# Sample attention of a hybrid decoder: key transposes placed between low passes, ten blocks loaded early, and three orders rewritten

## The reference

```python
s = jnp.einsum('bqhd,bkhd->bhqk', qi, k, preferred_element_type=jnp.float32) * scale
s = s + fi.transpose(0, 2, 1)[..., :, None] - fk_t[..., None, :]
mask = k_pos[None, :] <= pi[:, None]
s = jnp.where(mask, s, -jnp.inf)
p = jax.nn.softmax(s, axis=-1)
return jnp.einsum('bhqk,bkhd->bqhd', p.astype(v.dtype), v)
```

## Time and profile before

| | |
|---|---|
| median of 3 runs | 3514.9 us (3512.66 to 3516.16) |
| the profiled execution's own time | 3511.37 us |
| its span, first to last instruction | 3509.6 us |
| mean granted TensorE clock | 0.984 |
| `third_pass` of the first and the last chunk | start 2182.0 and 2962.4 us |
| busy share of the span | PE 96%, DVE 63%, ACT 51%, POOL 47% |

### The profile page before, as it was taken

The page is one execution under the profiler, slowest core; times in us unless marked ns, Lnnn a source line. Parts: engine busy times, 40 slices in busy tenths (PEclk is TensorE's granted clock), DMA queues, the critical chain, the costliest instruction groups (busy, mean ns, idle before and its releaser), DMA issues. The chain is left out here.

```text
span 3509.6 us, 54504 instructions
## 1 busy us (share of the span) xinstructions
PE 3369.2 (96%) x17111; PEld 2664.7 (76%) x17111; DVE 2194.4 (63%) x3610; ACT 1782.2 (51%) x3705; POOL 1663.9 (47%) x1239
## 2 busy tenths in 40 slices
PE   7899999999999999998999998999999998899999
PEld 6678887788787878886677676777777776778787
DVE  3425566777555556554777773888888887544432
ACT  4411222554423474645677776777777775311222
POOL 2411314153455354210688876777777777222100
PEclk9999999999999999998999999999999999999999
DMA  7878787888888887888011115999999996544422
GB/s 263 314 223 280 227 262 250 275 309 282 268 272 267 280 279 255 250 243 229 13 29 45 43 37 179 345 345 345 347 346 344 347 352 238 207 162 165 145 87 84
DMA packets 426005, 810.17 MB, mean 231 GB/s; under 512 B 97741, under 2 KB 119157, under 8 KB 425738
## 3 DMA queue, kind: packets, MB, share of 16 engines
q1 hardware_dynamic: 413650, 799.67, 68.3%
q10 hardware_dynamic: 11520, 5.12, 0.5%
q0 software_dynamic: 576, 2.10, 0.2%
HBM read 674.11 MB, written 132.67 MB: 230 GB/s over the span
## 5 line engine op out<-in xcount | busy, mean ns | idle before, releaser
L1495 PE MATMUL prj_z_ps<-prj_w_hi,prj_h_ring 128*128 128x512 f32 x1792 | 724.2, 404 | 11.1 <-DMA prj_h_ring<-hops_scratch 6.6
L1497 PE MATMUL prj_z_ps<-prj_w_hi,prj_h_ring 128*128 128x512 f32 x1792 | 703.3, 392 | 0.0
L1496 PE MATMUL prj_z_ps<-prj_w_lo,prj_h_ring 128*128 128x512 f32 x1792 | 701.6, 391 | 0.0
L1928 POOL TENSOR_TENSOR pa_p_lo<-pa_probs,pa_p_hi 128x512 fp32r<-128x512 f32 (+1 forms) x320 | 370.6, 1178 | 111.3 <-ACT pa_p_hi L1940 107.3
L1495 PEld LDWEIGHTS prj_z_ps<-prj_w_hi,prj_h_ring 128*128 128x128 f32 x1792 | 339.0, 189 | 80.8 <-issue 7.0
L2566 DVE TENSOR_TENSOR sa_kT_lo<-sa_t_ps,sa_kT_hi 128x512 fp32r<-128x512 f32 x512 | 334.1, 682 | 100.1 <-ACT sa_kT_hi L2457 97.8
L1497 PEld LDWEIGHTS prj_z_ps<-prj_w_hi,prj_h_ring 128*128 128x128 f32 x1792 | 338.2, 189 | 74.7
L1496 PEld LDWEIGHTS prj_z_ps<-prj_w_lo,prj_h_ring 128*128 128x128 f32 x1792 | 339.3, 189 | 66.6
L2436 POOL TENSOR_TENSOR sa_v_lo<-shared_v_early,sa_v_hi 128x1024 fp32r<-128x1024 f32 x130 | 310.5, 2411 | 102.1 <-DVE sa_v_hi L2572 101.8
L2436 POOL TENSOR_TENSOR sa_v_lo<-sa_v_late,sa_v_hi 128x1024 fp32r<-128x1024 f32 x126 | 301.2, 2412 | 82.1 <-DVE sa_v_hi L2572 82.0
L2457 ACT CAST sa_kT_hi<-sa_t_ps 128x512 fp32r<-128x512 f32 x512 | 278.2, 595 | 75.2 <-PE sa_t_ps L2720 69.7
(11 more groups left out here) (439 smaller groups left out, 7413.3 us busy)
## 6 DMA issues: line engine op xcount, KB each, us to landing
prj_h_ring<-hops_scratch SPq DMA_DIRECT2D x448, 512.0 KB, 4.6
arena_k_raw<-in_cache_k_dram SPq DMA_DIRECT2D x512, 256.0 KB, 4.1
shared_v_early<-in_cache_v_dram SPq DMA_DIRECT2D x260, 256.0 KB, 4.4
sa_v_late<-in_cache_v_dram SPq DMA_DIRECT2D x252, 256.0 KB, 4.4
z_scratch<-prj_z_sb SPq DMA_DIRECT2D x224, 256.0 KB, 5.5
prj_raw<-in_w_main_dram SPq DMA_DIRECT2D x104, 256.0 KB, 5.9
...
```

What stands on the lines that cost most here:

```text
L1495: pe.matmul(out, h[:, 0, k], hi, start=(k == 0), stop=False)
L1496: pe.matmul(out, h[:, 0, k], lo, start=False, stop=False)
L1497: mm = pe.matmul(out, h[:, 1, k], hi, start=False, stop=(k == HK - 1))
L1928: pool.tensor_tensor(p_lo[:, s % P_RING, 0:w], probs[:, s % P_RING, 0:w], p_hi[:, s % P_RING, 0:w].bitcast(F32), ALU.subtract).then_inc(pl ...
```

## The change

The loops of `attend_sample` are written in another order, V's ring shrinks from six chunks to four and K's grows from three to six, and one subtraction changes its engine in three chunks.

PE: the passes of a chunk are no longer alternated high and low. `score_high` makes four passes with `kT_hi`, then `score_low_and_turn` alternates the four passes with `kT_lo` with the four transposes of page 1 of the next chunk. `weigh_high` makes four passes with `v_hi`; the four with `v_lo` come one turn later (`WEIGH_LOW` is 5), at the start of the turn, alternating with the transposes of page 0. Pages 2 and 3 are turned in blocks of four.

ACT: `exp` moves from behind `high(g, 3)` to behind `high(g, 0)`, and the four `high` are spread out.

DVE: `reduce`, `swap` and `running` stand together at the start of the odd turns, and `low_keys` of page 0 follows them.

SP: 16 pages of V (4 chunks, into the tiles of the prompt's even heads) and 12 more of K (3 chunks, where V's were) are loaded in `attend_prompt`, after the 12 of K that were there: ten chunk loads in place of six. In the loop V is issued two chunks behind K. In the last three chunks POOL makes half of `v_lo` and DVE the other half. In the profile the rings will be named `v_ring` and `k_early`.

```diff
 class Shared:
+    V_RING = 4
...
+        even = one("even", [P, 4, SEQ], F32R)
+        self.even = [even[:, n] for n in range(4)]
+        self.v_ring = one("v_ring", [P, self.V_RING, CHUNK_PAGES, D_A])
...
             def begin_values():
+                sp.wait_ge(st_done, (HEADS - 1) * N_FIN)
...
                 if pair == HEADS // 2 - 1:
                     begin_sample()
+                    begin_values()
                     for g in range(GROUPS):
                         store(pair, slice(QG * g, QG * (g + 1)), GROUPS + g + 1)
                         if g == 1:
-                            begin_values()
+                            more_keys()
...
-    RING, V_RING = arena.RING, 2 * arena.RING
+    RING, V_RING, BEHIND = 2 * arena.RING, Shared.V_RING, 2
...
+            def load_both(g, n):
+                load_k(g, n % RING)
+                load_v(g - BEHIND, (n - BEHIND) % V_RING)
...
             def low_values(w):
                 pool.wait_ge(vhi_ready, w + 1)
-                for half in range(2):
+                for half in range(1 if is_last(w) else 2):
...
@@ @block.scalar, in the loop
                 if is_chunk(g):
                     high(g, 0)
-                    high(g, 1)
+                if odd and is_seg(s):
+                    exp(s)
...
                 if is_chunk(g - 1):
                     place(g - 1)
+                if is_chunk(g):
+                    high(g, 1)
+                if is_chunk(g - 1):
                     move(g - 1)
...
                 if is_chunk(g):
                     high(g, 2)
-                    high(g, 3)
-                if odd and is_seg(s):
-                    exp(s)
                 if is_chunk(g - 1):
                     fetch(g - 1)
                     take(g - 1)
+                if is_chunk(g):
+                    high(g, 3)
...
@@ @block.vector
+                if is_last(w):
+                    dve.wait_ge(vhi_ready, w + 1)
+                    at = slice(CP // 2, CP)
+                    dve.tensor_tensor(v_lo[:, w % 2, at], v_of(w)[:, at], v_hi[:, w % 2, at].bitcast(F32),
+                                      ALU.subtract).then_inc(vlo_last, 1)
...
                 if odd and is_seg(s):
                     reduce(s)
-                if is_chunk(g):
-                    low_keys(g, 0)
-                if odd and is_seg(s):
                     swap(s)
-                if is_chunk(g):
-                    low_keys(g, 1)
+                    running(s)
...
-                if odd and is_seg(s):
-                    running(s)
...
+                if is_chunk(g):
+                    low_keys(g, 0)
                 if is_chunk(g - 3):
                     high_values(g - 3)
...
                 if is_chunk(g):
+                    low_keys(g, 1)
                     low_keys(g, 2)
-                    low_keys(g, 3)
                 if not odd and is_seg((g - 6) // 2):
                     keep((g - 6) // 2)
+                if is_chunk(g):
+                    low_keys(g, 3)
...
@@ @block.tensor
+            def score_low_and_turn(g):
+                n, slot = g // CHUNKS, g % 2
+                pe.wait_ge(klo_ready, g * CP + CP)
+                if is_chunk(g + 1):
+                    may_turn(g + 1, 1)
+                for pair in range(PAIRS):
+                    if is_chunk(g + 1):
+                        turn_pair(g + 1, 1, pair)
+                    mm = pe.matmul(s_ps[0:R, slot], q_pair(n, pair)[:, 0:R], kT_lo[:, slot, pair], start=False, stop=(pair == PAIRS - 1),
+                                   skip_group_check=True)
+                mm.then_inc(scored, 1)
...
```

More of the change, by code:

```diff
@@ L20 @@
+import math
 from contextlib import ExitStack
@@ L2151, in maximum @@
                     o = max_ps[:, n % 2, 0:w]
-                    mm = pe.matmul(o, qA[:, h % 2, i * P:end], kA[:, h % 2, c * BLK:c * BLK + w], start=True, stop=not diag)
+                    mm = pe.matmul(o, qA[h % 2][:, i * P:end], kA[h % 2][:, c * BLK:c * BLK + w], start=True, stop=not diag)
                     if diag:
@@ L2666, in _ @@
                     reduce(s)
-                if is_chunk(g):
-                    low_keys(g, 0)
-                if odd and is_seg(s):
                     swap(s)
-                if is_chunk(g):
-                    low_keys(g, 1)
+                    running(s)
+                if not odd and is_seg(s):
+                    low(s, 0)
+                    low(s, 1)
+                    if first_seg(s):
+                        low_new(s // PER)
                 if g == 1:
@@ L2681, in _ @@
                     dve.tensor_copy(lift_r[:], lift[:]).then_inc(lift_ready, 1)
-                if odd and is_seg(s):
-                    running(s)
-                if not odd and is_seg(s):
-                    low(s, 0)
-                    low(s, 1)
-                    if first_seg(s):
-                        low_new(s // PER)
+                if is_chunk(g):
+                    low_keys(g, 0)
                 if is_chunk(g - 3):
@@ L2730, in first_passes, with turn_pair, turn, q_pair @@
-            def first_passes(g):
+            def turn_pair(g, j, pair):
+                mm = pe.transpose(t_ps[:, j % 2, pair * PAGE:(pair + 1) * PAGE], k_raw[g % RING][:, j, pair * P:(pair + 1) * P], ident[:])
+                if pair == PAIRS - 1:
+                    mm.then_inc(turned, 1)
+            def turn(g, j):
+                may_turn(g, j)
+                for pair in range(PAIRS):
+                    turn_pair(g, j, pair)
+            def q_pair(n, pair):
+                return q_of(n)[:, pair * P:(pair + 1) * P]
@@ L2739, in score_new @@
                 pe.wait_ge(mask_ready, 1)
-                score(n, x_ps[:, 0:SAMPLE], lambda pair: kn_hi[:, pair], lambda pair: kn_lo[:, pair]).then_inc(new_scored, 1)
+                out = x_ps[:, 0:SAMPLE]
+                for pair in range(PAIRS):
+                    q = q_pair(n, pair)
+                    pe.matmul(out, q, kn_hi[:, pair], start=(pair == 0), stop=False, skip_group_check=True)
+                    mm = pe.matmul(out[0:R], q[:, 0:R], kn_lo[:, pair], start=False, stop=(pair == PAIRS - 1), skip_group_check=True)
+                mm.then_inc(new_scored, 1)
             def third_pass(g):
```

177 lines of the change are left out of this document (101 added, 76 removed).

## The result

| kernel | median us (lowest to highest) | ratio to before, 95% interval |
|---|---|---|
| before | 3515.5 (3512.7 to 3521.0) | |
| changed | 3586.9 (3581.8 to 3592.3) | 1.020, 1.018 to 1.022 |

The account below looks back on a forecast made before the run. POOL's subtractions and DVE's `v_hi`, each waiting for the other, were taken to bound the kernel at 11.87 us per pair of chunks. 38.4 - 1.8 + 10 - 2 = +45 us on 3511.4 gave 3556, so 3560; range 3538 to 3590.

Parts of the forecast that it names:

- the likeliest case: The kernel gets slower as forecast, DVE's later `v_hi` costing time in each pair of chunks: 3540 to 3576 us, 67%.
- the chain behind `exp` outgrows its cover: Rival: ACT, PE and DVE work after `exp` outlasts POOL's subtractions, +0.25 to +0.5 us a pair, 3576 to 3592, 20%.
- The hold and POOL's ring: DVE's `running` held until POOL's subtraction ends, `low_keys` then delays `v_hi` and POOL: 12.47 us a pair against 11.87.
- POOL's starts would alternate 6.6 and 5.9: Sign of being right: in mid-sequence POOL's starts lie 6.6 and 5.9 us apart in turn.
- For 64 pairs +38.4: Sample attention loop: +0.60 us in each pair of chunks, +38.4 us for 64 pairs.
- The even turn stays at 5.89: Only the odd turn of a pair of chunks gets longer; the even one keeps 5.89 us.
- so this chain just fits ... and costs nothing: Work from `exp` on lets the even turn's `v_hi` start at 11.3, POOL ends at 11.40: 0.1 us spare, no cost.
- Ends of sequences, +10: DVE's `weighted`, `total` and divide held by POOL 1.9, 1.3 and 2.2 us: +1.4 us, seven times, +10.
- no extra at the ends: The reason given for the range's lower end, 3538: sequence ends add nothing.
- Transposes between low passes: PE: a transpose between two low passes taken at 0.07 us against 0.11 in a block; buys nothing in time.
- Last three chunks, -2: POOL has 2.4 us less work in each, DVE one instruction more: -1.2 to -3.6 us, taken as -2.
- Early loads, 0: Four more chunk loads issued before the sample attention: 0, since nobody waits for DMA.

Follow-up runs that it names:

- a_p3: The changed kernel with a second buffer for the second half of `p_both`, so `halves(1)` does not wait for the same turn's low weighing: 3574.9 us, 1.016.
- a_exp: The changed kernel with one edit on ACT, `exp` behind `high(2)` instead of behind `high(0)`: 3570.1 us, 1.016.

## Why the prediction was right, and where it was off

The direction and the range (3538 to 3590) held. The number, 3560, was 27 us low, and the likeliest case (3540 to 3576) was missed. What happened is the rival with 20%, "the chain behind `exp` outgrows its cover" (3576 to 3592), but not by the causes that it names and not at its price: the pair is 13.15 us, 0.68 above the forecast's 12.47, where the rival had 0.25 to 0.5. That the time still lies between 3576 and 3592, and inside the range, is in part luck: the +38.4 was too high, the even turn and the starts of sequences too low.

- *The hold and POOL's ring.* Right: `v_hi` ends 6.57 us after the one before in the odd turn (2466.99, 2473.57) against a forecast of 6.58, and the pair is 12.46 against 12.47 where the step was made alone. The sign that POOL's starts would alternate 6.6 and 5.9 did not come: they are 6.57 and 6.59 apart.
- *"For 64 pairs +38.4".* Mis-sized: in the kernel before it is worth 23 us by itself. I took the sequence's start for regular pairs plus 3.3 us of extras on top; in fact the first three pairs hide what POOL's ring loses.
- *"The even turn stays at 5.89", "so this chain just fits ... and costs nothing".* This is the step that failed. The even turn's `v_hi` starts 11.94 us after that of the even turn before has ended (2466.99 to 2478.93), not 11.3. 0.36 of the 0.64 are a wait that I had not in the chain: `halves(1)`, and through it both `low`, wait for the low weighing, which the change had moved one turn later. I priced that move only for the last chunk. a_p3 takes it away and the pair falls by 0.39. The rest are sizes: `high(1)` 0.60 for 0.49, three steps of 0.35 for 0.30 (the transposes, below), 0.15 between `low_keys(2)` and PE for 0.06. The forecast had 0.1 us of slack for a sum of eleven terms.
- *Ends of sequences, +10.* The holds are as forecast: `weighted` 1.92, `total` 1.29 and the division 2.08 us (medians) for 1.9, 1.3 and 2.2. What they do is not: the three pairs from chunk 1 to 7 cost 4.5 us more in each sequence; the forecast had 1.4 and three times 0.60, 3.2.
- *The range.* Its lower end, 3538, is explained by "no extra at the ends", but 3560 less 10 is 3550.
- *Transposes between low passes.* Taken at 0.07 us, with "nearer 0.07 than 0.11" as a sign; in the trace 0.11: two transposes with their low passes take 0.68 (2476.32 to 2477.00), a low pass alone 0.23. In blocks they took 0.11 too. PE's need stayed at 11.8 a pair, so PE's new order had nothing to give. The tile of the scores in the changed kernel has the loads of the high and of the low passes:

```profile
L2771 PEld LDWEIGHTS sa_s_ps<-sa_kT_hi,sa_q_both x512: 186/188/192, 2174.0 to 3036.7; 128*128 128x128 f32 x171
...
L2781 PEld LDWEIGHTS sa_s_ps<-sa_kT_lo,sa_q_both x512: 133/134/138, 2175.0 to 3037.6; 128*64 128x64 f32 x171
```

 The Trainium skill ("TensorE: Matmul & The Clock Gate", section "LDWEIGHTS") gives load time by columns, half for 64 of what 128 take. Here 64 columns take 134 ns and 128 take 188, and a transpose's 128 columns 141 (the mean of L2753 on the profile's page): the saving that the rule gives a transpose beside a narrow load does not appear.
- *Last three chunks, -2.* 3.5 in the trace. *Early loads, 0.* 0 within some 6 us.

Counted by the table, a sequence pays 10.6 us more; eight sequences, the first and last not whole, make the 80.

What stays open: the starts of sequences, 4.5 of these 10.6 us, whose cause is read from one trace and was not tested. Then whether there is an order of ACT and DVE with which PE's new order runs at its 11.8: with every one tried the pair took 12.76 or more. And why a_exp alone stops at 12.80: `halves(1)` still waits 0.67 us in its trace, but no run tells that wait from those of PE.
